# Every second gate and up pair of two groups as seven block products instead of eight

## The reference, cut to what matters

```
def swiglu(x, w_gate, w_up, w_down):
    return (jax.nn.silu(x @ w_gate) * (x @ w_up)) @ w_down
...
for l in range(DEPTH):
    x = x + 0.5 * swiglu(rmsnorm(x, norm_w[l, 0]), ffn_w_gate[l, 0], ffn_w_up[l, 0], ffn_w_down[l, 0])
...
    x = x + 0.5 * swiglu(rmsnorm(x, norm_w[l, 2]), ffn_w_gate[l, 1], ffn_w_up[l, 1], ffn_w_down[l, 1])
out = rmsnorm(x, final_norm_w)
```

## Time and profile before

| | |
|---|---|
| median of the runs | 2326.1 us |
| the profiled execution, its own time | 2327.64 us |
| its span, first to last instruction | 2325.9 us |
| mean granted TensorE clock | 0.995 of 2.4 GHz |
| TensorE busy | 2289.0 us (98%), 17176 matmuls |
| VectorE busy | 1073.5 us (46%) |
| ScalarE busy | 677.3 us (29%) |
| DMA | 201.29 MB, mean 87 GB/s |

### The profile page before, as it was taken

One profiled execution on the slowest core, in us unless ns is written; L12 is line 12 of the kernel. 1 busy time (PEld: TensorE's weight loads), 2 busy tenths in 40 slices (PEclk: granted clock), 3 DMA queues, 4 the chain that ended last, 5 costly groups with the idle time before them and its releaser, 6 DMA issues.

```text
span 2325.9 us, 39302 instructions
## 1 busy us (share of the span) xinstructions
PE 2289.0 (98%) x17176; PEld 2266.9 (97%) x17176; DVE 1073.5 (46%) x1387; ACT 677.3 (29%) x830; POOL 45.7 (2%) x50
## 2 busy tenths in 40 slices
PE   7999999999999999999999999999999999999997
PEld 7999999999999999999999999999999899999997
DVE  5433424585555433434543333354765463334245
ACT  4212212354533222212322222233422432222122
POOL 0000000001100000000000000000011100000000
PEclk9999999999999999999999999999999999999999
DMA  5222222224332222222222222222123322222221
GB/s 176 91 80 83 86 78 61 85 89 137 114 98 78 89 87 84 79 91 63 93 80 91 73 90 84 75 77 91 55 87 97 99 73 90 89 74 80 83 75 57
DMA packets 72552, 201.29 MB, mean 87 GB/s; under 512 B 7268, under 2 KB 26980, under 8 KB 72448
## 3 DMA queue, kind: packets, MB, share of 16 engines
q1 hardware_dynamic: 72448, 199.80, 26.8%
HBM read 187.82 MB, written 11.95 MB: 86 GB/s over the span
## 4 chain that ended last, share of the span: by engine, by line
PE 94%; DVE 3%; ACT 1%; issue 0%; POOL 0%; DMA 0%; DVEq 0%; SPq 0%; ACTq 0%; POOLq 0%
PE ps L447 84%; PE ps L672 4%; PE ps L527 1%; PE ps L703 1%; PE ps L692 1%; DVE w_lo L1548 1%; PE ps L706 0%; PE ps L722 0%; PE ps L536 0%; PE ps L715 0%; PE ps L550 0%; PE ps L716 0%; DVE x L2196 0%; PE ps L498 0%; POOL scratch L1528 0%
## 5 line engine op out<-in xcount | busy, mean ns | idle before, releaser
L447 PE MATMUL ps<-xn_hi,w_hi 128*128 128x288 f32 x3328 | 718.9, 298 | 11.8 <-DVE w_lo L1548 11.4
L447 PE MATMUL ps<-xn_hi,w_lo 128*128 128x288 f32 x3328 | 713.8, 296 | 0.0
L447 PE MATMUL ps<-xn_lo,w_hi 128*128 128x288 f32 x3328 | 713.1, 296 | 0.0
L447 PEld LDWEIGHTS ps<-xn_hi,w_hi 128*128 128x128 f32 x3328 | 537.2, 189 | 19.9 <-issue 18.0
L447 PEld LDWEIGHTS ps<-xn_hi,w_lo 128*128 128x128 f32 x3328 | 537.1, 189 | 0.0
L447 PEld LDWEIGHTS ps<-xn_lo,w_hi 128*128 128x128 f32 x3328 | 537.1, 189 | 0.0
L1104 ACT ACTIVATE w_hi<-raw 128x1024 fp32r<-128x1024 f32 x332 | 331.7, 1047 | 351.7 <-PE ps L447 327.3
L1548 DVE TENSOR_TENSOR w_lo<-raw,w_hi 128x1024 fp32r<-128x1024 f32 x332 | 391.4, 1220 | 41.2 <-ACT w_hi L1104 39.0
L447 PE MATMUL ps<-h_lo,w_hi 128*128 128x288 f32 x1616 | 351.4, 297 | 4.1 <-DVE h_hi L1861 4.1
L447 PE MATMUL ps<-h_hi,w_hi 128*128 128x288 f32 x1616 | 350.9, 296 | 1.4 <-DVE w_lo L1548 1.4
L1593 DVE TENSOR_TENSOR scratch<-ps,rstd 128x576 f32<-128x576 f32 x88 | 66.7, 758 | 537.0 <-PE ps L447 534.0
(11 more groups left out here) (239 smaller groups left out, 1565.1 us busy)
## 6 DMA issues: line engine op xcount, KB each, us to landing
raw<-in_w_gate SPq DMA_DIRECT2D x88, 512.0 KB, 3.7
raw<-in_w_up SPq DMA_DIRECT2D x88, 512.0 KB, 4.5
raw<-in_w_down SPq DMA_DIRECT2D x64, 512.0 KB, 3.7
raw<-in_w_mix SPq DMA_DIRECT2D x64, 512.0 KB, 4.2
raw<-in_w_down SPq DMA_DIRECT2D x32, 384.0 KB, 3.5
state_s<-in_state_c SPq DMA_DIRECT2D x4, 1024.0 KB, 6.4
out_c_s<-state_s SPq DMA_DIRECT2D x4, 1024.0 KB, 4.5
state_s<-in_state_g SPq DMA_DIRECT2D x4, 1024.0 KB, 7.1
```

What stands on the lines that cost most here:

```text
L447: ins = nc.tensor.matmul(o, a, b[:, c] if c is not None else b, start=first and j == 0, stop=last and j == 2)
```

## The change

In groups 1 and 2 of each feed-forward block, the odd pair (gate and up block of one hidden tile) is computed another way. The product of the weights (rows: gate, up; columns: even k tiles, odd k tiles) and the activations (rows: even k tiles, odd k tiles; columns: first and second token half) is a 2 by 2 block product. Before it takes 8 block products; now it takes 7, each over 4 k tiles and 288 columns, on sums of blocks: S1 to S4 of weights, and four sums t of activations. The sums of weights are made for every such pair on VectorE, from `raw`, into T(6) to T(9), and split in high and low parts like any weights; w_hi and w_lo of slots 2 and 3 now hold four "units" of 4 tiles each, and units 0, 1 and 2 are overwritten within the pair. The sums of activations are made once for each feed-forward block, in the D phase of group 0, into `th_hi` and `th_lo`, which lie over v_tok and the states. The products accumulate in banks 4 to 7, and between them ScalarE copies bank 5 three times; VectorE adds the copies.

```diff
+        th_hi = inner.enter_context(nc.sbuf_tensor("th_hi", [P, 4, 4, HALF_TOK], f32r))
...
+            def seven_pair(ph, i, t_wait=False):
+                pair, w = ph["base"] + 2 * i + 1, ph["seven"] + i
...
+                def product(u, bank, right, first):
+                    for k in range(KT_X // 2):
+                        ws = slice(k * P, (k + 1) * P)
+                        wh, wl = unit(w_hi, u)[:, ws], unit(w_lo, u)[:, ws]
+                        xh, xl = right(k)
+                        for j, (a, b) in enumerate(((wh, xh), (wh, xl), (wl, xh))):
+                            ins = nc.tensor.matmul(ps[:, bank, FIRST], a, b, start=first and k == 0 and j == 0,
+                                                   stop=k == KT_X // 2 - 1 and j == 2, skip_group_check=True)
+                    return ins
...
+                pe.wait_ge(unit_lo, 5 * w + 1)
+                product(0, 5, x_tiles(even, 0), True).then_inc(product_done, 1)
+                pe.wait_ge(lo_done, 2 * pair + 1)
+                product(1, 4, x_tiles(odd, 0), True).then_inc(product_done, 1)
+                if t_wait:
+                    pe.wait_ge(t_lo_done, 4 * (ph["ffn"] + 1))
+                pe.wait_ge(unit_lo, 5 * w + 2)
+                pe.wait_ge(copy_done, 3 * w + 1)
+                product(2, 5, t_tiles(1), False).then_inc(product_done, 1)
+                pe.wait_ge(unit_lo, 5 * w + 3)
+                product(3, 6, t_tiles(2), True).then_inc(product_done, 1)
+                pe.wait_ge(unit_lo, 5 * w + 4)
+                pe.wait_ge(copy_done, 3 * w + 2)
+                product(0, 5, t_tiles(0), False).then_inc(product_done, 1)
+                pe.wait_ge(lo_done, 2 * pair + 2)
+                product(1, 7, t_tiles(3), True).then_inc(product_done, 1)
+                pe.wait_ge(unit_lo, 5 * w + 5)
+                pe.wait_ge(copy_done, 3 * w + 3)
+                return product(2, 5, x_tiles(odd, 1), False)
...
-                        ins = feature_pair(ph, i, half)
+                        if half and seven:
+                            ins = seven_pair(ph, i, t_wait=ph["group"] == 1)
+                        else:
+                            ins = feature_pair(ph, i, half)
```

ScalarE, for an iteration of groups 1 and 2:

```diff
+            def units_early(ph, i):
+                pair, w = ph["base"] + 2 * i + 1, ph["seven"] + i
+                act.wait_ge(pe_done, pair - 1)
+                act.wait_ge(raw_full[2], 8 * (pair - 1) + 16)
+                unit_high(0, raw_tiles(0, 0)).then_inc(unit_hi, 1)
+                unit_high(1, raw_tiles(0, 1)).then_inc(hi_done, 1)
+                act.wait_ge(sum_ready, 4 * w + 3)
+                unit_high(2, by_tile(S2)).then_inc(unit_hi, 1)
+                unit_high(3, by_tile(S3)).then_inc(unit_hi, 1)
...
+                def between():
+                    act.wait_ge(product_done, 6 * w + 1)
+                    product_copy(P1_COPY)
+                    unit_high(0, by_tile(S1)).then_inc(unit_hi, 1)
+                evac_g(ph, i, 0, between)
+                act.wait_ge(product_done, 6 * w + 2)
+                act.wait_ge(raw_full[3], 8 * (pair - 1) + 16)
+                unit_high(1, raw_tiles(1, 1)).then_inc(hi_done, 1)
+                act.wait_ge(product_done, 6 * w + 3)
+                product_copy(U2_COPY)
+                unit_high(2, by_tile(S4)).then_inc(unit_hi, 1)
+                act.wait_ge(product_done, 6 * w + 5)
+                product_copy(U4_COPY)
+                split_next(j, i, 1)
```

VectorE, in `seven_half` after `units_early` (S1, S3, S2, low part 0, S4, low parts 1, 2, 3) and `evac_g` of the even pair, in which the low part of S1 stands between T(2) and h_lo:

```diff
+                dve.wait_ge(hi_done, 2 * pair + 2)
+                unit_low(1, raw_tiles(1, 1)).then_inc(lo_done, 1)
+                dve.wait_ge(copy_done, 3 * w + 1)
+                dve.wait_ge(product_done, 6 * w + 2)
+                V.tensor_tensor(first_gate, ps[:, 4, FIRST], P1_COPY, ALU.add).then_inc(part_ready, 1)
+                dve.wait_ge(unit_hi, 5 * w + 5)
+                unit_low(2, by_tile(S4)).then_inc(unit_lo, 1)
...
+                dve.wait_ge(copy_done, 3 * w + 3)
+                V.tensor_tensor(second_up, ps[:, 6, FIRST], U4_COPY, ALU.add).then_inc(part_ready, 1)
+                split_next(j, i, 1)
+                dve.wait_ge(part_ready, 5 * w + 3)
+                V.tensor_tensor(second_up, second_up, rstd[:, SECOND], ALU.mult).then_inc(part_ready, 1)
+                dve.wait_ge(product_done, 6 * w + 6)
+                V.tensor_tensor(first_up, ps[:, 7, FIRST], third, ALU.add).then_inc(part_ready, 1)
...
+            def evac_seven(ph, i):
+                dve.wait_ge(pe_done, pair + 1)
+                V.tensor_tensor(T(0)[:, SECOND], ps[:, 5, FIRST], rstd[:, SECOND], ALU.mult).then_inc(tg_ready, 1)
+                dve.wait_ge(part_ready, 5 * w + 5)
+                V.tensor_tensor(T(1)[:, FIRST], T(1)[:, FIRST], rstd[:, FIRST], ALU.mult).then_inc(psum_free, 1)
+                hidden_rows(q, m, pair)
...
                 for pp in range(4):
                     split_next(j, pp // 2, pp % 2)
+                    if ph["group"] == 0:
+                        t_sums(ph, pp)
                     add_to_x(ph, pp, 0.5, final=ph["last"])
+                    if ph["group"] == 0:
+                        t_low(ph, pp)
```

More of the change, by code:

```diff
@@ L35, in schedule @@
 def schedule():
-    out, pair, hidden = [], 0, 0
+    out, pair, hidden, seven = [], 0, 0, 0
     for layer in range(2):
@@ L48, in schedule @@
                 out.append(dict(kind="G", pairs=k, base=pair, ffn=ffn, norm=norm, k=KT_X, k0=k0,
-                                group=g, hidden=hidden))
-                pair, hidden = pair + k, hidden + k
+                                group=g, hidden=hidden, seven=seven))
+                pair, hidden, seven = pair + k, hidden + k, seven + (k // 2 if g else 0)
                 out.append(dict(kind="D", pairs=4, base=pair, ffn=ffn, norm=norm, k=k, k0=k0,
@@ L94 @@
 LOG_D_MAX = float(np.log(D_MAX))
+UNIT = KT_X // 2 * P
 CONV_S = TAIL + DEC_SEQ
@@ L244, in late_weights, with unit, raw_tiles, by_tile @@
             return tensor[:, :, :].rearrange("p k n -> p (k n)")[:, at:at + n]
+        def unit(buf, u):
+            return buf[:, 2 + u // 2, u % 2 * UNIT:(u % 2 + 1) * UNIT]
+        def raw_tiles(blk, odd):
+            return raw[:, 2 + blk, :].rearrange("p (k o n) -> p k o n", o=2, n=P)[:, :, odd, :]
+        def by_tile(ap):
+            return ap.rearrange("p (k n) -> p k n", n=P)
+        S1, S2, S3, S4 = (T(t)[:, 0:UNIT] for t in (8, 9, 7, 6))
+        FIRST, SECOND = slice(0, HALF_TOK), slice(HALF_TOK, TOK)
+        P1_COPY, U2_COPY, U4_COPY = T(3)[:, FIRST], T(3)[:, SECOND], T(4)[:, FIRST]
         PIECES = ((0, CUT), (CUT, TOK))
@@ L503, in phase @@
                 consumer = ph["kind"] == "G" and ph["group"] == 0
+                seven = ph["kind"] == "G" and ph["group"] > 0
                 def iteration(i, first_norm=False, bank_wait=True):
@@ L1115, in split_next, with unit_high, product_copy, seven_half @@
                     split(ph, i + 1, 0)
+            def unit_high(u, src):
+                return nc.scalar.activation(by_tile(unit(w_hi, u)), src, ACT.Copy)
+            def units_early(ph, i):
[7 more added lines that the diff above has]
+                unit_high(3, by_tile(S3)).then_inc(unit_hi, 1)
+            def product_copy(dst):
+                return nc.scalar.activation(dst, ps[:, 5, FIRST], ACT.Copy).then_inc(copy_done, 1)
+            def seven_half(j, ph, i):
+                pair, w = ph["base"] + 2 * i + 1, ph["seven"] + i
+                def between():
[12 more added lines that the diff above has]
+                split_next(j, i, 1)
+            def t_high(ph, pp):
+                act.wait_ge(t_ready, 4 * ph["ffn"] + pp + 1)
+                nc.scalar.activation(th_hi[:, :, pp, :], T2(5).rearrange("p a (c n) -> p (a c) n", c=2), ACT.Copy)\
+                    .then_inc(t_hi_done, 1)
             def xn_high(norm, m):
@@ L1149, in iteration, with seven_iteration @@
                         evac_g(ph, i, half)
+                def seven_iteration(i):
+                    units_early(ph, i)
+                    seven_half(j, ph, i)
+                    evac_g(ph, i, 1)
+                if ph["group"]:
+                    iteration = seven_iteration
                 iteration(0)
@@ new lines, in evac_seven @@
+            def evac_seven(ph, i):
+                q, m = ph["hidden"] + 2 * i + 1, 2 * i + 1
+                pair, w = ph["base"] + m, ph["seven"] + i
+                dve.wait_ge(pe_done, pair + 1)
[3 more added lines that the diff above has]
+                hidden_rows(q, m, pair)
@@ new lines, in t_sums @@
+            def t_sums(ph, pp):
+                f = ph["ffn"]
+                even, odd = T(3), T(4)
+                V.tensor_tensor(even, xn_hi[:, 2 * pp, :].bitcast(f32), xn_lo[:, 2 * pp, :].bitcast(f32), ALU.add)
+                own(V.tensor_tensor(odd, xn_hi[:, 2 * pp + 1, :].bitcast(f32), xn_lo[:, 2 * pp + 1, :].bitcast(f32),
+                                    ALU.add))
```

(15 more changed lines are left out.)

60 lines of the change are left out of this document (58 added, 2 removed).

## The result

The changed kernel takes 2272.2 us (median of four executions, 2271.7 to 2274.8), the one before beside it 2326.1: ratio 0.977, 95% interval 0.976 to 0.978. Its profiled execution took 2274.84 us, with a span of 2273.1.

The account below looks back on a forecast made before the run. TensorE, 98% busy, was taken to bound the kernel. -48.6 (fewer matmuls) + 3.9 (late h_lo and last down phase) + 0.9 (thin place) = -43.8 us, giving 2282.3 us from the 2326.1 median; forecast range 2276 to 2290, 8 in 10 2276 to 2300.

Parts of the forecast that it names:

- The gain: 28 odd pairs with 84 matmuls instead of 96, at 0.1317 us: 11.06 against 12.80 us, 48.6 us saved.
- The thin place: w_lo for the even pair after a new pair, met by only 0.15 us; late in 12 pairs, +0.9 us.
- Rival 1: The next even pair's w_lo is late everywhere, 0.3 to 1.0 us a pair: 2290 to 2310 us; chance 0.2.
- h_lo late at the 6 k down starts: VectorE finishes odd pairs late, so h_lo comes 1.0 us later at three group 2 down starts.
- The last down phase: Its start waits for h_hi, w_hi and w_lo, which move by 1.0 us: stall from 1.4 to 2.4 us.
- rival 3: Clock falls at the new gaps, 1.55 us a fall: 2288 us at four stalls, 2326 at every pair; chance 0.02.
- Satisfied waits: Waits on TensorE that are met in time cost it nothing measurable.
- TensorE's queue: A new pair has 12 waits instead of 3, but the queue runs ahead: zero, bounds 0 and 25 us.
- activation sums: VectorE's added work in the first down phase, about 4.6 us a pair, delays nothing: zero.
- early units: Three weight sums and low parts, made during the even pair, end at 10 us against 12.8 when wanted.
- Rival 2: TensorE's queue doesn't run ahead through the products; each of 7 boundaries costs a restart: 2330 to 2340 us; chance 0.05.
- the better case: A whole-kernel time better than 2276 us; chance 0.04.

Follow-up runs that it names:

- f1: The changed kernel with products 3 to 6 reading halves of xn in place of the activation sums th: 2285.9 us (one execution).
- g3: The changed kernel with th_lo moved up by 64 bytes in each partition, nothing else: 2284.7 us (one execution).
- i1: The changed kernel with one w_lo subtraction later on VectorE and ten filling matmuls in the last down phase's wait, no other added matmul: 2266.8 us, ratio 0.975.
- h1: The changed kernel with added shifted-operand matmuls in group 0 and the 6 k down phases, and ten filling the last down phase's wait: 2262.8 us, ratio 0.972.
- e3: The kernel before with two more already satisfied waits ahead of each block of the odd pairs of groups 1 and 2: 2326.1 us (one execution).
- h5: As h1, with one w_lo subtraction later on VectorE and the added matmuls' operand starting at a multiple of 128 bytes: 2258.0 us, ratio 0.971.
- g5: The changed kernel with xn_hi and xn_lo both moved to odd multiples of 64 bytes: 2266.5 us (one execution).
- g4: The changed kernel with xn_lo moved to an odd multiple of 64 bytes, th_lo as before: 2271.4 us (one execution).
- e1: The kernel before with odd pairs of groups 1 and 2 taking one token half, so one bank, at a time: 2326.7 us, ratio 1.000.
- e2: The kernel before with all gate, up and down pairs one bank at a time, last down phase aside: 2347.8 us (two executions), ratio 1.009.

## Why the forecast was wrong, by its steps

- **The gain, 28 x 1.74 = 48.6.** 336 matmuls fewer, as counted. The new pairs took 11.10 to 11.11 us, forecast 11.06: 0.1322 a matmul and not 0.1317, 1.3 us less gain. The step that failed is one that I did not write down: the sum leaves every unchanged pair at 12.80, so it puts their change at nothing without a reason. In each FFN ten of them (three even pairs and four down pairs of group 1, three even pairs of group 2) ran at 12.48: 10 x 0.32 x 4 = 12.8 us. All of the miss of 10.1 us is in it, less what follows. f1 and g3, which are after in all but what or where th is read, have 2285.9 and 2284.7, 2 to 4 us above the forecast: the better time is luck with one address, which the forecast had no part in. No row of before shows a long stretch at 0.1300, but the spread of 0.1311 to 0.1334 in the earlier trace rows for one instruction was a sign that spacing is no constant, and I took it for the weights' place.
- **The thin place, +0.9.** It held everywhere, with the room forecast. Timelines of after:

```profile
214.11 2.00 ACT L1177 ACTIVATE w_hi<-raw 128x1024 fp32r<-128x1024 f32 x2
...
215.19 2.36 DVE L1678 TENSOR_TENSOR w_lo<-raw,w_hi 128x1024 fp32r<-128x1024 f32 x2 [0.49 <-ACT w_hi L1177]
```

```profile
216.66 0.30 PE L527 MATMUL ps<-xn_hi,w_lo 128*128 128x288 f32 x1
216.79 0.42 PE L472 MATMUL ps<-xn_hi,w_hi 128*128 128x288 f32 x2
```

  The first w_lo ends at about 216.41, 0.25 us ahead of the load that needs it (0.13 us before 216.79), forecast 0.15. The copy took 0.41 and not the 0.43 assumed. Rival 1 is out, and the 0.9 us was not spent.
- **h_lo late at the 6 k down starts, 3 x 1.0.** As forecast: 1.18 us where 1.2 stood, and the first pair took 10.7 us against 9.8, 3 x 0.9. i1 confirms the cause: with one w_lo taken out from ahead of it, h_lo is no longer waited for, and 0.30 us for that w_lo remain.
- **The last down phase, +1.0.** The stall grew as forecast (2.31 against 2.4), but the last down phase and the end by 1.9 us and not 1.0, since the clock fell behind it; h1 shows that cause by filling the wait. That is rival 3 at one of the four stalls, and at the price that it gave for a fall, 1.5 us. It had been put aside because 1.41 us of idle left the clock at 1.00; at 2.31 it did not.
- **Satisfied waits, TensorE's queue, activation sums, early units: zero.** Right. L527 has no idle, e3 shows no cost for more waits, and the pairs of group 0 and of its down phase, where the activation sums are made, take 12.80 in f1 and in after as in before. Rival 2 is out. Through the seven new pairs of group 1 and 2 the granted clock was 1.00 as well, so the Trainium skill's failure mode of the clock by cycled banks (TensorE: Matmul & The Clock Gate, A second HAM failure mode: psum-queue depth-cycling) did not show there.
- **Sum.** From the profiled execution of before, 2327.6: the forecast had -43.8, and it became -52.8. The difference of 9.0 is 12.8 (rhythm), 0.9 (thin place) and 0.2 (the down starts) on the one side, 1.3 (new pairs), 0.9 (the last down phase and the end) and 2.9 (mixers) on the other: 8.8, and 0.2 is left over. The mixers were put at nothing; which executions fall to half clock there the forecast couldn't say.

Also the range was too narrow on that side: the better case had a chance of 0.04, with no mechanism in it.

**What stays open.** What the quick rhythm is. Shown: it needs no change of the instructions that run in it. In after it lasts over pairs, phases and met waits until TensorE really waits. Reading th brought it in every FFN of after, h1 to h5 and i1, and not when th_lo was moved by 64 bytes or not read. Added matmuls can start and end it, differently from one FFN to the next at the same place. Bank order, count and met waits don't start it. Not shown: that an odd multiple of 64 bytes is the rule. g3, g5 and the second iterations of the 6 k down phases speak for it; g4, where the down pairs of group 1 stay at 12.80 though th_lo and xn_lo both lie so, and h5, whose group 0 is quick without one, speak against it. The experiments on addresses are one execution each, and no other distance than 64 bytes was tried for th_lo. So the 12.4 us are shown to hang on the place of th_lo, and why they do was not found.

## What to carry to other kernels

Cost the unchanged work as well: a change of the stream can move the spacing of identical matmuls behind it by 2.5%, so compare pieces of the merged chain with equal counts before a gain or a loss is put down to the change's own mechanism, and undo the parts one at a time. Where one wait on the ending chain is lengthened, look for the clock behind it; ten matmuls that nobody reads, put into the wait, were worth 1.5 us here. Before a difference of a few us between single executions is explained, take out the stretches at half clock that lie elsewhere. On an engine that does both, put what the next phase waits for first and part an operation pair whose second half is wanted later.

## What the runs showed of the hardware

- The same 128x128 by 288 matmul with its own weight load repeats every 0.1333 us (starts 131, 131, 131, 140 ns apart) or every 0.1300 (128, 132), both at a granted clock of 1.00; at 2.4 GHz that is 320 and 312 clocks. Which one is a state that lasts for hundreds of microseconds (1152 matmuls in 153.59 or 149.76 us).
- One bank for 24 matmuls in a row gives 12.72 us for 96, two banks in turn 12.80 (e1, e2).
- After an idle of 1.41 us of TensorE the granted clock was 1.00, after one of 2.31 us 0.57 for the next 4 us. In e2 it stayed at 1.00 after idles of 1.17 us and was 0.57 for 4 us after one of 1.96.
- The mixers took 596.3 us with no time at half clock (h5) and 603.8 with 17.1 us of it (after).
- A copy of 128x288 from PSUM on ScalarE takes 0.41 us (mean of 84).
